# Two transformer blocks on one core: TensorE waits idle for each normalization in place of running matmuls on constants

## What is computed

```
def rms_norm(x, gain):
    xf = x.astype(jnp.float32)
    y = xf * lax.rsqrt(jnp.mean(xf * xf, axis=-1, keepdims=True) + EPS)
    return (y * gain.astype(jnp.float32)).astype(x.dtype)
...
def first_block(...):
        hn = rms_norm(x, norm1_g[l])            # norm 0
        proj = hn @ w_in[l]
        ...                                     # two attentions on parts of proj, two gates
        x = x + mixed @ w_out[l]
        x = x + conv_glu(rms_norm(x, norm2_g[l]), ...)                        # norm 1
...
def second_block(...):
        h = rms_norm_2(x, norm_mix_g[layer])    # norm 2
        z = h @ w_in[layer]
        ...                                     # a gated recurrence, an attention, two gates
        x = x + merged @ w_out[layer]
        hf = rms_norm_2(x, norm_ffn_g[layer])   # norm 3
        x = x + (jax.nn.silu(hf @ w_ffn_gate[layer]) * (hf @ w_ffn_up[layer])) @ w_ffn_down[layer]
        hp = rms_norm_2(x, norm_ple_g[layer])   # norm 4
        x = x + jax.nn.sigmoid(hp @ w_ple_gate[layer]) * (p[layer] @ w_ple_proj[layer])
```

## Time and profile before

| what | value |
|---|---|
| runs | 1740.63 us median of 3 (1739.75 to 1742.53) |
| profiled execution | span 1742.2 us; its own time isn't listed beside it (of the three runs only 1742.53 is longer than this span) |
| TensorE busy | 1708.9 us, 98% |
| ScalarE, VectorE, GpSimd busy | 38%, 34%, 44% |
| mean granted TensorE clock | 0.994 of full |
| matmuls on constants | 38 records of 592 ns |

### The profile page before, as it was taken

The page is one execution under the profiler, slowest core; times in us unless marked ns, Lnnn a source line. Parts: engine busy times, 40 slices in busy tenths (PEclk is TensorE's granted clock), DMA queues, the critical chain, the costliest instruction groups (busy, mean ns, idle before and its releaser), DMA issues.

```text
span 1742.2 us, 22714 instructions
## 1 busy us (share of the span) xinstructions
PE 1708.9 (98%) x7752; PEld 1347.5 (77%) x7752; DVE 595.7 (34%) x963; ACT 666.9 (38%) x1151; POOL 766.3 (44%) x605
## 2 busy tenths in 40 slices
PE   8999999999999999999999999999999999999998
PEld 6776777677788888888678877777778888888877
DVE  4065513324343333300466432554423111110043
ACT  5243364233354444322443434433334333332242
POOL 7444432224364444444457423322336444444442
PEclk9999999999999999999999999999999999999999
DMA  4421121112243333333222223221223333333212
GB/s 147 125 90 43 49 73 56 48 55 85 61 120 97 97 96 97 96 92 97 73 73 74 67 61 112 64 55 54 74 79 104 97 97 96 110 95 97 91 55 91
DMA packets 103207, 145.58 MB, mean 84 GB/s; under 512 B 11093, under 2 KB 56894, under 8 KB 102990
## 3 DMA queue, kind: packets, MB, share of 16 engines
q1 hardware_dynamic: 102958, 142.30, 28.0%
q10 hardware_dynamic: 160, 2.11, 0.3%
HBM read 142.24 MB, written 2.13 MB: 83 GB/s over the span
## 4 chain that ended last, share of the span: by engine, by line
PE 90%; DVE 4%; ACT 2%; issue 2%; POOL 1%; DMA 1%; DVEq 0%; ACTq 0%; SPq 0%
PE bank L1484 77%; PE bank L1427 4%; PE bank L1404 3%; PE bank L1412 1%; DVE work L1320 1%; PE bank L1609 1%; PE bank L1582 1%; POOL w_lo L617 1%; POOL h_lo L467 1%; ACT L799 1%; ACT h_hi L859 0%; DVE h_lo L467 0%; PE bank L1630 0%; DMA w_raw<-in_w_in 0%; PE bank L1644 0%
## 5 line engine op out<-in xcount | busy, mean ns | idle before, releaser
L617 POOL TENSOR_TENSOR w_lo<-w_raw,w_hi 128x512 fp32r<-128x512 f32 x516 | 680.5, 1326 | 823.0 <-ACT w_hi L792 820.4
L792 ACT ACTIVATE w_hi<-w_raw 128x512 fp32r<-128x512 f32 x516 | 318.8, 629 | 687.5 <-PE bank L1484 612.4
L1484 PE MATMUL bank<-h_hi,w_lo 128*128 128x512 f32 x1376 | 551.7, 401 | 7.6 <-ACT hk L882 2.9
L1484 PE MATMUL bank<-h_hi,w_hi 128*128 128x512 f32 x1376 | 538.5, 391 | 0.0
L1484 PE MATMUL bank<-h_lo,w_hi 128*128 128x512 f32 x1376 | 538.0, 391 | 0.0
L1484 PEld LDWEIGHTS bank<-h_hi,w_lo 128*128 128x128 f32 x1376 | 259.7, 189 | 91.2 <-issue 23.6
L1484 PEld LDWEIGHTS bank<-h_hi,w_hi 128*128 128x128 f32 x1376 | 259.5, 189 | 55.8
L1484 PEld LDWEIGHTS bank<-h_lo,w_hi 128*128 128x128 f32 x1376 | 259.9, 189 | 54.5 <-issue 2.9
L1484 PE MATMUL bank<-g_hi,w_lo 128*128 128x512 f32 x352 | 138.8, 394 | 0.0
L1484 PE MATMUL bank<-g_hi,w_hi 128*128 128x512 f32 x352 | 138.7, 394 | 0.0
L1484 PE MATMUL bank<-g_lo,w_hi 128*128 128x512 f32 x352 | 138.7, 394 | 0.0
(11 more groups left out here) (262 smaller groups left out, 1772.7 us busy)
## 6 DMA issues: line engine op xcount, KB each, us to landing
w_raw<-in_w_in SPq DMA_DIRECT2D x168, 256.0 KB
w_raw<-in_w_ffn_up SPq DMA_DIRECT2D x88, 256.0 KB
w_raw<-in_w_ffn_down SPq DMA_DIRECT2D x88, 256.0 KB
w_raw<-in_w_ffn_gate SPq DMA_DIRECT2D x88, 128.0 KB
w_raw<-in_w_ffn_up SPq DMA_DIRECT2D x88, 128.0 KB
w_raw<-in_w_out SPq DMA_DIRECT2D x32, 256.0 KB
w_raw<-in_w_branch_b SPq DMA_DIRECT2D x16, 256.0 KB
w_raw<-in_w_branch_a SPq DMA_DIRECT2D x16, 256.0 KB
```

What stands on the lines that cost most here:

```text
L617: e.tensor_tensor(w_lo[:, pos % SPLIT_SLOTS, :], w_raw[:, pos % RAW_SLOTS, :], w_hi[:, pos % SPLIT_SLOTS, :].bitcast(F32), ALU.subtract).t ...
L792: e.activation(w_hi[:, pos % SPLIT_SLOTS, :], w_raw[:, r, :], ACT.Copy).then_inc(hi_full, 1)
L1484: mm = e.matmul(ps[banks + n][:, :], l, r, start=k == 0 and i == 0, stop=k == p.kc - 1 and i == 2)
```

## The change

TensorE's part of the step "warm" keeps its wait for bank 5 and still raises bank_free[5], by an instruction that does nothing else. The matmuls between are gone. The other engines' programs and the order of all other steps are the same. Lines below 1523 stand two lines higher in the changed kernel.

```
                 elif what == "warm":
-                    bank = bank_wait(e, x)
-                    for i in range(4 if x[1] else 7):
-                        mm = e.matmul(bank[:, :], ident[:, :], chunk_start[:, :], start=True, stop=True)
-                    mm.then_inc(bank_free[5], 1)
+                    bank_wait(e, x)
+                    e.nop().then_inc(bank_free[5], 1)
                 elif what == "vec":
```

## The result

| | median | range | runs |
|---|---|---|---|
| before | 1741.18 us | 1739.49 to 1742.85 | 20 |
| after | 1743.96 us | 1739.91 to 1746.57 | 20 |

The medians differ by 2.8 us. The ratio after to before is 1.0017, with a 95% interval from 1.0010 to 1.0023, that is 1.7 to 4.0 us slower.

What follows compares the result with a forecast made beforehand. TensorE, busy 98% of the span, was taken to bound the kernel. Norms 0 to 3 summed 0.5 + 2.2 - 1.6 + 2.2 = +3.3 us; median plus that is 1743.9, taken as 1744.2, range 1741.0 to 1747.3.

Steps and rivals of the forecast that it cites:

- The matmuls on constants delay nothing today: Ahead of norms 0 to 3, the constant passes end 0.2 to 0.3 us before the data; removing them gains 0 directly.
- The clock falls in all four norms: TensorE would idle 8.07 us in norm 0 and 3.86 in norms 1 to 3, so the clock falls at each.
- Rival 1: The clock holds in norms 1 to 3 and falls only in norm 0: 1741.1 us, chance 0.08.
- The price of a fall, 2.2 us a norm: Matmuls after a norm's restart run at the low clock, losing between 1.6 and 2.7 us; 2.2 taken, 2.3 for norm 0.
- Norm 0, +0.5: qB loses 2.3 us; kB's wait for ScalarE's copy of qB covers 1.76, leaving +0.5.
- Norm 2, 0 and -1.6: hf's loss of 2.2 us vanishes in the later 2.90 us wait (0); the fall at 868.83 goes too (-1.6).
- Rival 2: The fall near 868 gives nothing back, recurring after the change or absent from the median run: +4.9, 1745.5 us, chance 0.15.
- How I read the profiled execution against the runs: Profiled span 1742.2 is 1.6 us above the runs' median 1740.63, as much as one fall of the clock.
- Rivals 3 and 4: Waits at 43.91 and 868.32 cover nothing: 1749.5, chance 0.08; or constants delay real matmuls at low clock: 1740.4, chance 0.05.
- Rival 4: In norm 0 at low clock, 14 constant passes end 5.3 us after the data; change saves 3.5: 1740.4, chance 0.05.

## Why the prediction was right, and where it was not

The slowdown came, +2.8 us where the sum had +3.3. The larger chance, 0.53, had gone to more than 0.2% slower, and it came out just within. That 1744.2 lies 0.2 from the measured median is in part luck: the median of before moved up by 0.55 with more runs, and the terms' errors pull both ways, as follows.

*The matmuls on constants delay nothing today.* Right. Every restart of after still waits for h_lo, and a delay of TensorE ahead of up1 (2.05 us, seven in norm 1) is charged in full, so one that existed before would have shown as a gain.

*The clock falls in all four norms.* Right: at 17.50, 471.48, 843.53 and 1307.74. Rival 1 (it holds in norms 1 to 3) is out.

*The price of a fall, 2.2 us a norm.* Right in the mean: 2.7 and 1.4 in the profile of after, 1.3 and 1.6 in that of the kernel without constants in norms 1 and 3, 4.2 for the pair in that kernel's runs against my 4.4. Both patterns that I had read from the earlier trace rows appeared, the long one where the fall came 0.9 us before the restart (471.48 to 472.38), the short one where it came 0.2 before (1307.74 to 1307.91). The boundary that I had drawn, before or after the restart, is therefore not sharp.

*Norm 0, +0.5.* Right, as far as two profiles go: kB was 0.15 later in after and 0.9 later in the kernel without constants in norm 0. I had booked 2.3 lost and 1.76 covered; 1.5 was lost in the one and 2.6 in the other. The runs give 0.0 plus or minus 1.6 and can't tell.

*Norm 2, 0 and -1.6.* The cover is right: three kernels show it (after, the one without constants in norm 2, and the one with seven there, whose clock is never low in hf). The relief of 1.6 was sized too large. It assumed the fall in each run of before, and 1.6 for it: it stands in five of six profiles, and costs some 1.35 from norm 2's restart to norm 3's, so 1.1 in the mean. Three measurements of it (norm 2 bare, norm 2 with seven, the wait filled) give 0.3, 0.9 and 0.9 faster, each plus or minus 1.6, a mean of 0.7, which agrees. Rival 2 had 0 here, and the profiles speak against it; the runs alone don't settle it. With 0.5, 4.2 in place of 4.4, and 1.1 in place of 1.6 my sum would have been 3.6 instead of 3.3; the medians say 2.8, and the ratio's interval holds all three.

*The rule on idle gaps.* The Trainium skill (TensorE: Matmul & The Clock Gate, "Why this matters for your kernels") advises against idle gaps over about 3 us. As advice against this change it was right. As a line below which nothing happens it is too generous here: the profiles have five falls behind waits of 2.77 to 2.94 us ahead of hq and seven behind 2.3 us ahead of pgate.

*How I read the profiled execution against the runs.* Wrong. I set the span of 1742.2 beside the median of 1740.63 and called the difference one fall. With the 1.7 us that lie around a span, the profiled execution of before took some 1743.9, 2.7 us above the median of its 20 runs. It was an unlucky one, with falls at 152 (long), 326, 868 and 1694. That didn't hurt the forecast only because I then left the span and added to the median.

*Rivals 3 and 4.* Nothing is covered: out, by norms 0 and 2. Constants that hold up real work at a low clock: not seen; each profile has the clock high from 10.7 us or earlier. Rival 4's working has a slip: 6.28 - 0.59 over 13 steps is 0.438 us and not 0.427, which would put the end of the slow passes 0.3 us later; nothing hangs on it.

## What to carry to other kernels

Filler, that is work whose result nobody reads, on an engine whose clock falls after idle time is worth what the next stretch behind it can't hide: price it by the low clock after the restart, not by the filler, and ask for each place whether a wait follows before the end of the dense work. Filler pays where dense work follows for long (norms 1 and 3) and little or nothing where the engine would soon wait anyway (norms 0 and 2). Two further waits together gave 1.4 us when filled, so look for waits that have none. Where falls of the clock come and go from run to run, compare some twenty runs of each kernel and cut the profiles at points that both share, since the difference of two single spans here even had the wrong sign. Stretches without a fall of their own repeat to a few hundredths of a microsecond: norm 1's restart to norm 2's took 369.11 to 369.15 us in eight profiles.

## What the runs showed of the hardware

- The clock didn't fall at the same point of the same wait: 4.4 us into norm 0's idle stretch in after (13.15 to 17.50), 2.8 us into norm 1's, 3.0 into norm 2's and 3.5 into norm 3's. The low level then lasted 3.41, 6.83 or, once, 10.24 us.
- The same code falls in one execution and not in another: with 2.3 us of waiting ahead of pgate the clock fell near the restart in seven profiles, before among them, and stayed high in three, after among them.
- Idle stretches of 1.98 us went without a fall in one profile and cost nothing there, while that kernel's runs were 2.1 us slower on average: seven of 12 had a lower mean clock (0.992 to 0.995 against 0.997 or 0.998) and were 3.5 us or more slower than the other five.
- The scatter of this kernel's runs, some 3 to 5 us, is about two to three falls of the clock wide; 1.6 us is one short fall. A run's time goes with its mean granted clock: the correlation is -0.93 over 35 runs of before.
